# Seven products in place of eight for three of eight k-tile pairs in the first two column blocks of the last gate projection

## The reference, cut to what matters

```python
h = x
xn = rms_norm(h, attn_norm); proj = xn @ W_in
h = h + concat(gated_deltanet(...), moba_attention(...)) @ W_o
hn = rms_norm(h, ffn_norm)
h = h + (silu(hn @ w_gate) * (hn @ w_up)) @ w_down        # 2048 x 5632 and back
gate = sigmoid(rms_norm(h, ple_norm) @ w_ple_gate)         # 2048 x 2048
h = h + gate * (p @ w_ple_proj)                            # p 256 x 256, w 256 x 2048
```

## Time and profile before

| | us |
|---|---|
| median of 3 runs | 1311.76 (1311.75 to 1312.54) |
| the profiled execution | 1312.5 |
| its span, first to last instruction | 1310.8 |
| TensorE busy | 1302.5 (99%) |
| VectorE busy | 1025.2 (78%) |
| ScalarE busy | 704.7 (54%) |

### The profile page before, as it was taken

One profiled execution on the slowest core, in us unless ns is written; L12 is line 12 of the kernel. 1 busy time (PEld: TensorE's weight loads), 2 busy tenths in 40 slices (PEclk: granted clock), 3 DMA queues, 4 the chain that ended last, 5 costly groups with the idle time before them and its releaser, 6 DMA issues.

```text
span 1310.8 us, 18558 instructions
## 1 busy us (share of the span) xinstructions
PE 1302.5 (99%) x6595; PEld 1076.9 (82%) x6595; DVE 1025.2 (78%) x1381; ACT 704.7 (54%) x937; POOL 53.7 (4%) x71
## 2 busy tenths in 40 slices
PE   9999999999999999999999999999999999999998
PEld 8788888887888887888888888888888888888887
DVE  6578886788586668889888988679888997968554
ACT  6576444543455565555555654445555555555643
POOL 4003000221000000000000000000000000000000
PEclk9999999999999999999999999999999999999999
DMA  8555554455434555665666556566666656556563
GB/s 271 177 174 164 159 147 129 145 149 152 144 119 145 177 177 164 205 211 184 194 198 207 192 193 216 185 211 184 198 205 209 190 182 209 193 178 208 193 199 139
DMA packets 126204, 238.37 MB, mean 182 GB/s; under 512 B 9711, under 2 KB 10786, under 8 KB 126138
## 3 DMA queue, kind: packets, MB, share of 16 engines
q1 hardware_dynamic: 126106, 237.48, 56.8%
q10 hardware_dynamic: 32, 0.01, 0.0%
HBM read 235.36 MB, written 2.10 MB: 181 GB/s over the span
## 4 chain that ended last, share of the span: by engine, by line
PE 98%; DVE 1%; ACT 0%; issue 0%; DMA 0%; DVEq 0%; ACTq 0%
PE pair L627 16%; PE pair L629 16%; PE pair L628 16%; PE pair L908 11%; PE pair L909 11%; PE pair L910 11%; PE bg L908 2%; PE bg L909 2%; PE bg L910 2%; PE bg L748 2%; PE bg L818 2%; PE bg L685 1%; PE bg L903 1%; PE bg L799 0%; PE bg L660 0%; DVE w_lo L1493 0%
## 5 line engine op out<-in xcount | busy, mean ns | idle before, releaser
L1493 DVE TENSOR_TENSOR w_lo<-raw,w_hi 128x1024 fp32r<-128x1024 f32 x442 | 531.8, 1222 | 179.2 <-ACT w_hi L1099 177.4
L1099 ACT ACTIVATE w_hi<-raw 128x1024 fp32r<-128x1024 f32 x401 | 417.1, 1055 | 250.5 <-PE pair L629 139.9
L627 PE MATMUL pair<-w_hi,xT_hi 128*128 128x512 f32 x780 | 314.6, 403 | 0.0
L629 PE MATMUL pair<-w_hi,xT_lo 128*128 128x512 f32 x780 | 305.0, 391 | 0.0
L628 PE MATMUL pair<-w_lo,xT_hi 128*128 128x512 f32 x780 | 304.4, 390 | 0.0
L629 PEld LDWEIGHTS pair<-w_hi,xT_lo 128*128 128x128 f32 x780 | 146.5, 188 | 31.5
L627 PEld LDWEIGHTS pair<-w_hi,xT_hi 128*128 128x128 f32 x780 | 146.9, 188 | 28.9
L628 PEld LDWEIGHTS pair<-w_lo,xT_hi 128*128 128x128 f32 x780 | 147.0, 188 | 27.4
L1373 ACT ACTIVATE w_hi<-raw 128x1024 fp32r<-128x1024 f32 x41 | 43.6, 1062 | 134.7 <-DVE raw L1823 134.7
L908 PE MATMUL pair<-w_hi,actT_hi 128*128 128x512 f32 x296 | 115.9, 392 | 0.0
L910 PE MATMUL pair<-w_hi,actT_lo 128*128 128x512 f32 x296 | 115.3, 389 | 0.0
(11 more groups left out here) (351 smaller groups left out, 1886.0 us busy)
## 6 DMA issues: line engine op xcount, KB each, us to landing
raw<-in_w_in_dram SPq DMA_DIRECT2D x112, 512.0 KB, 3.7
raw<-in_w_gate_dram SPq DMA_DIRECT2D x88, 512.0 KB, 4.6
raw<-in_w_up_dram SPq DMA_DIRECT2D x88, 512.0 KB, 4.5
raw<-in_w_down_dram SPq DMA_DIRECT2D x88, 512.0 KB, 4.8
raw<-in_w_o_dram SPq DMA_DIRECT2D x32, 512.0 KB, 3.9
raw<-in_w_ple_gate_dram SPq DMA_DIRECT2D x32, 512.0 KB, 4.1
raw<-in_w_ple_proj_dram SPq DMA_DIRECT2D x4, 512.0 KB, 4.1
h<-in_x_dram SPq DMA_DIRECT2D x3, 512.0 KB, 8.0
```

The source lines that it names most:

```text
L627: mm(banks[t][:], hi[:, ts], wh, start=first, stop=False)
L629: m = mm(banks[t][:], lo[:, ts], wh, start=False, stop=last)
L1099: f(w_hi[j % RING][:], raw[j % RING][:], ACT.Copy).then_inc(hi_ready, 1)
L1493: v.tensor_tensor(w_lo[j % RING][:], raw[j % RING][:], w_hi[j % RING][:].bitcast(F32), ALU.subtract).then_inc(lo_ready, 1)
```

## The change

Groups 4, 5 and 6 of the gate projection's first two column blocks are computed with seven products for each pair of units. The units of these blocks come in the order `PG_SEQ`: block 0 groups 0, 1, 2, 3, 7 (G0 to G4), then the pair of group 4 for both blocks (G5, G6), block 1 group 0, the pair of group 5 (G8, G9), block 1 group 1, the pair of group 6 (G11, G12), block 1 groups 2, 3, 7 (G13 to G15). Blocks 2 and 3 stay plain. The steps hB of groups 4, 5 and 6 get the longer form with sums and differences. Those of groups 4 and 5 move from `U_PP - 2` to P1 (`U_PP + 1`). The sums of block 0 and of block 1 are finished at G12 and G15, and the multiply and add behind the sigmoid at G13 and G17.

```diff
-            at[(U_DB + FF_B * 8 // KU + 3, U_DB + FF_B * 8 // KU + 5, U_PP - 2, U_PP + 3)[n]][g].append(("hB", 2 * n + g))
+            at[(U_DB + FF_B * 8 // KU + 3, U_DB + FF_B * 8 // KU + 5, U_PP + 1, U_PP + 3)[n]][g].append(("hB", 2 * n + g))
...
+PG_MIXED = (4, 5, 6)
+PG_PLAIN = [g for g in range(UPB) if g not in PG_MIXED]
+PG_SEQ = ([(0, g) for g in PG_PLAIN] + [(0, PG_MIXED[0]), (1, PG_MIXED[0]), (1, PG_PLAIN[0])]
+          + [(0, PG_MIXED[1]), (1, PG_MIXED[1]), (1, PG_PLAIN[1])]
+          + [(0, PG_MIXED[2]), (1, PG_MIXED[2])] + [(1, g) for g in PG_PLAIN[2:]])
+PG_END = PG_SEQ.index((1, PG_MIXED[-1]))
...                                                     SyncE
+            for j, (side, g) in enumerate(PG_SEQ):
+                if j >= RING and PG_SEQ[j - RING] in [(0, m) for m in PG_MIXED]:
+                    sp.wait_ge(t4_ready, MIX_PG + PG_MIXED.index(PG_SEQ[j - RING][1]) + 1)
+                    fetch(j, w_pg, KU * g, side * CB)
+                else:
+                    load(U_PG + j, j, w_pg, KU * g, side * CB)
...                                                     TensorE, a mixed pair
+                    if first:
+                        pe.wait_ge(pair_free[1], 2 * ((B_PG + 1) // 2))
+                        for n in PG_MIXED:
+                            wait_read(pe, ("hB", n))
...
+                    use(u)
+                    product(bg[0][:], xT_hi[:, k0, a0], xT_lo[:, k0, a0], gh[:, 0, :], gl[:, 0, :], first, last)
+                    product(pair[0][0][:], xT_hi[:, k1, a0], xT_lo[:, k1, a0], gh[:, 1, :], gl[:, 1, :], False,
+                            last).then_inc(unit_used, 1)
+                    use(u + 1)
+                    product(bg[3][:], E_hi[:, q, 0, :], E_lo[:, q, 0, :], uh[:, 0, :], ul[:, 0, :], first, last)
+                    product(pair[1][0][:], E_hi[:, q, 2, :], E_lo[:, q, 2, :], uh[:, 1, :], ul[:, 1, :], first,
+                            False).then_inc(unit_used, 1)
+                    pe.wait_ge(t3_lo_ready, MIX_PG + q + 1)
+                    product(bg[2][:], E_hi[:, q, 3, :], E_lo[:, q, 3, :], t_hi[:, 2, :], t_lo[:, 2, :], first, last)
+                    pe.wait_ge(t24_lo_ready, MIX_PG + q + 1)
+                    product(bg[1][:], E_hi[:, q, 1, :], E_lo[:, q, 1, :], t_hi[:, 0, :], t_lo[:, 0, :], first, last)
+                    product(pair[0][1][:], xT_hi[:, k1, a1], xT_lo[:, k1, a1], t_hi[:, 1, :], t_lo[:, 1, :], False,
+                            last).then_inc(t_used, 1)
...                                                     ScalarE, step hB of groups 4, 5, 6
+                        if b - 1 in groups:
                             wait_read(act, (step, b - 1))
+                        elif step == "hB":
+                            act.wait_ge(down_sum, 4 * SUMS)
...                                                     (two scaled copies to xg as in hA)
+                        if step == "hB":
+                            f(xT_hi[:, 2 * b:2 * b + 2, :], xg[:], ACT.Copy).then_inc(x_hi, 2)
+                            act.wait_ge(form_ready, 4 * (c + 1))
+                            f(E_hi[:, q, :, :], F_raw[:], ACT.Copy).then_inc(form_rounded, 1)
+                            return
...                                                     ScalarE, the turns of P0 to G31
+                if side and g in PG_MIXED:
+                    split_mixed(u + LEAD, u + LEAD, MIX_PG + PG_MIXED.index(g) + 1, False)
+                elif u + LEAD < UNITS:
                     split(u + LEAD, u + LEAD)
                 for k in range(2):
                     for s in AT[u][k]:
...
                 if u < U_PG:
                     pp_end(u - U_PP)
                     continue
+                if u == U_PG + PG_END:
+                    act.wait_ge(t_used, MIX_PG + len(PG_MIXED))
+                    f(act_s[1][:], bg[0][:], ACT.Copy).then_inc(p1_copied, 1)
+                    for t in range(NT):
+                        act.wait_ge(gate_sum, 2 * (FF_A + FF_B) + t + 1)
+                        f(gate_s[t][:], gate_s[t][:], ACT.Sigmoid, scale=h_rs[1][:, t:t + 1]).then_inc(pair_free[0], 1)
...                                                     VectorE, step hB (behind F_raw as in hA)
+                        if step == "hB":
+                            v.tensor_tensor(xT_lo[:, 2 * b:2 * b + 2, :], xg[:], xT_hi[:, 2 * b:2 * b + 2, :].bitcast(F32), ALU.subtract)
+                            dve.wait_ge(form_rounded, c + 1)
+                            read_out(s, v.tensor_tensor(E_lo[:, q, :, :], F_raw[:], E_hi[:, q, :, :].bitcast(F32), ALU.subtract))
+                            return
...                                                     VectorE, the sums
+                if u == U_PG + PG_END:
+                    dve.wait_ge(p1_copied, done + 4 + 1)
...                                                     (six adds of 128 x 512: v_s, gate_s[0], u_s, gate_s[1], v_s, u_s)
+                if u == U_PG + PG_END + 1:
+                    finish(0, gate_s, pair_free[0], 2 * (B_PG // 2))
+                if u == U_PG + 2 * UPB - 1:
+                    wait_block(dve, u)
+                    dve.wait_ge(pg_parts, 2)
+                    for t, part in ((0, v_s), (1, u_s)):
+                        v.tensor_tensor(act_s[t][:], pair[1][t][:], part[:], ALU.add).then_inc(pair_free[1], 1)
+                if u == U_PG + 2 * UPB + 1:
+                    finish(1, act_s, pg_sig, 0)
```

More of the change, by code:

```diff
@@ L504, in _ @@
                 load(U_PP + b, b, w_pp, 0, b * CB)
-            with sp.Fori(0, 2) as i:
-                for j in range(2 * UPB):
-                    load(i * (2 * UPB) + (U_PG + j), j, w_pg, KU * (j % UPB), i * (2 * CB) + j // UPB * CB)
+            for j, (side, g) in enumerate(PG_SEQ):
[4 more added lines that the diff above has]
+                    load(U_PG + j, j, w_pg, KU * g, side * CB)
+            for j in range(2 * UPB, 4 * UPB):
+                load(U_PG + j, j, w_pg, KU * (j % UPB), j // UPB * CB)
             for b in range(3):
@@ L1053, in _ @@
                 down(ud, bd, n, n0, md, turn_last)
[L1055 to L1059, removed]
-            straight(U_PP, B_PP, 4, 1, lambda b, k: (pT_hi[:, k, :], pT_lo[:, k, :]))
-            straight(U_PG, B_PG, 3, UPB, normed)
+            straight(U_PP, B_PP, 4, 1, lambda b, k: (pT_hi[:, k, :], pT_lo[:, k, :]))
@@ new lines, in _ @@
+            a0, a1 = slice(0, P), slice(P, TOK)
+            pe.wait_ge(pair_free[0], 2 * (B_PG // 2))
+            for j, (side, g) in enumerate(PG_SEQ):
+                u = U_PG + j
+                k0, k1 = KU * g, KU * g + 1
+                if not side:
+                    wait_read(pe, ("hB", g))
+                if g in PG_MIXED:
+                    if side:
+                        continue
+                    q = PG_MIXED.index(g)
+                    first, last = q == 0, q == len(PG_MIXED) - 1
+                    if first:
+                        pe.wait_ge(pair_free[1], 2 * ((B_PG + 1) // 2))
+                        for n in PG_MIXED:
+                            wait_read(pe, ("hB", n))
+                    gh, gl = w_hi[j % RING], w_lo[j % RING]
+                    uh, ul = w_hi[(j + 1) % RING], w_lo[(j + 1) % RING]
+                    use(u)
[12 more added lines that the diff above has]
+                            last).then_inc(t_used, 1)
+                    continue
+                use(u)
+                for kk in range(KU):
+                    k = KU * g + kk
+                    wh, wl = w_hi[j % RING][:, kk, :], w_lo[j % RING][:, kk, :]
+                    end = side == 1 and j == len(PG_SEQ) - 1 and kk == KU - 1
+                    o = pair[side]
+                    product(o[0][:], xT_hi[:, k, a0], xT_lo[:, k, a0], wh, wl, not side and k == 0, end)
+                    last = product(o[1][:], xT_hi[:, k, a1], xT_lo[:, k, a1], wh, wl, k == 0, end)
+                    if kk == KU - 1:
+                        last.then_inc(unit_used, 1)
@@ L1064, in _ @@
+            straight(U_PG + 2 * UPB, B_PG + 2, 1, UPB, lambda b, k: (xT_hi[:, k, :], xT_lo[:, k, :]))
             last_pair = pair[(B_PG + 3) % 2]
@@ L1127, in post @@
                         act.wait_ge(x1_full, 1)
-                    if step == "hA" and b in MIXED:
-                        if b - 1 in MIXED:
+                    if b in {"hA": MIXED, "hB": PG_MIXED}.get(step, ()):
+                        groups = MIXED if step == "hA" else PG_MIXED
+                        if b - 1 in groups:
                             wait_read(act, (step, b - 1))
+                        elif step == "hB":
+                            act.wait_ge(down_sum, 4 * SUMS)
                         for kk in range(2):
@@ L1134, in post @@
                               scale=gains[:, col + k:col + k + 1]).then_inc(xg_ready, 1)
-                        q = MIXED.index(b)
-                        act.wait_ge(xg_ready, 2 * (q + 1))
+                        q = groups.index(b)
```

(55 more changed lines are left out.)

13 lines of the change are left out of this document (9 added, 4 removed).

## The result

| | us |
|---|---|
| median before | 1311.76 (6 runs, 1311.19 to 1312.54) |
| median after | 1317.17 (6 runs, 1316.0 to 1317.64) |
| ratio | 1.0042, 95% interval 1.0032 to 1.0051 |
| profiled execution after, its span | 1316.99, 1315.3 |

Slower, by 5.4 us; 4.06 were forecast. 1317.17 lies above the forecast's own range (1314.9 to 1316.7), inside the range for all (1313.2 to 1317.8), and nearest to rival C's 1317.5. The page of the kernel after, busy time and the last chain, against the earlier trace rows: nine matmuls fewer, and TensorE's share of the chain is 97% where it was 98%.

The account below looks back on a forecast made before the run. TensorE was taken to bound the kernel, its work and waits counting one for one. Terms -2.04 (matmuls) + 4.4 (wait) + 1.7 (clock) = +4.06 us gave 1315.8 us, own range 1314.9 to 1316.7, for all 1313.2 to 1317.8.

Parts of the forecast that it names:

- the forecast's own range: Whole kernel: 1314.9 to 1316.7 us around the forecast 1315.8, for start of the posts, handovers and clock; chance 0.65.
- the range for all: Whole kernel: 1313.2 to 1317.8 us over forecast and rivals, leaving out the no-wait rival and the slowest end.
- rival C: Behind P3's wait or at the sums: low clock twice as long, or waits at the sums; 1317.5 us, chance 0.15.
- What bounds the kernel: Whole kernel: TensorE, busy 1302.5 of 1310.8 us; work removed or waits added count one for one.
- Nine matmuls, 2.04 us: Gate phase's three mixed pairs: seven products instead of eight drop 9 matmuls of 0.2267 us, saving 2.04 us.
- The wait of 4.4 us: TensorE at P3's start: waits 4.4 us for ScalarE's copy of P1's banks behind two longer posts; bounds 2.2 and 6.7.
- The clock: Behind the wait at P3: TensorE's clock falls to half, losing 1.7 us more; bounds 0 and 3.4.
- my bound of 3.4 us: Behind the wait at P3: upper bound on the clock loss, low for twice the time.
- Splits and sums at nothing: Gate phase behind P3: VectorE's splits and sums keep ahead of TensorE; cost nothing, at most 0.5 us.
- The thinnest spot: Sums before G17: VectorE needs 10.2 us, TensorE wants G17 at 10.9; 0.7 us of cover.
- A (no wait): P3's start: ScalarE's copy comes in time, only the 9 matmuls count; 1309.7 us, chance 0.1.
- B (clock up): Behind P3's start: the wait comes but the clock stays at 2.4 GHz; 1314.1 us, chance 0.1.

Follow-up runs that it names:

- move only: Also called e3: kernel before the change, with hB steps of groups 4 and 5 moved to P1 in short form, eight products everywhere; 1311.77 us, ratio 0.9999.
- e4: Changed kernel with ScalarE's copies ahead of the posts, group 4's step three units before P0, group 5's behind P1's first k tile; 1310.29 us, ratio 0.9987.
- e10: The spread version of the changed kernel with only groups 4 and 5 through seven products, group 6 plain; 1310.89 us, ratio 0.9992.
- e9: Changed kernel with group 4's step three units before P0, ScalarE's copies still behind the posts; 98.58 us from P0 to the end.
- filler kernel with 18 matmuls: Changed kernel with 18 unused 512-column matmuls into a spare bank between P2 and P3; 1313.71 us, ratio 1.0014.
- 4 fillers: Changed kernel with 4 matmuls, results unused, in TensorE's gap ahead of P3; 1315.46 us, ratio 1.0027.
- e1: Changed kernel with ScalarE's copies of P units' banks put ahead of the hB posts of the same turn; 1313.66 us, ratio 1.0012.

## Why the prediction was right, and which term was too small

- **What bounds the kernel** held: TensorE's matmuls and its waits went into the time one for one. What came on top was the clock, and some tenths: 0.13 to 0.15 us for a restart behind a gap, 0.12 in "move only".
- **Nine matmuls, 2.04 us.** Shown by e4 (-1.98 us locally) and e10 (0.68 for each group).
- **The wait of 4.4 us.** 4.40 measured, twice. Step by step: the first post began 5.89 us after zero (5.9 to 6.1 forecast), the second 3.91 later (3.46 + 0.4), the copy 2.58 behind that (2.5), and ended 13.44 (13.45). VectorE's w_lo of G0 did hold up the first forms, to 7.18 us, 0.42 behind 5.89 + 0.87. e3 and e9 show that the length of the posts makes the wait, not the move.
- **The clock** fell, as forecast. Here a size was wrong: the term of 1.7 us. P3 took 2.90 us longer where I had 1.68, about 2.75 of it clock and 0.15 the restart. I had taken the loss from the one gap of half the length in the trace, where the clock was low for 3.4 us, all but a few hundredths of it behind the restart. Behind the new gap it was low for 6.8 us, in both profiles, of which 6.0 and 5.3 us lay behind the restart. That is the case of my bound of 3.4 us, "low for twice the time", and of the first half of rival C, which I had given 0.15. The sum with 2.90 in place of 1.7 is -2.04 + 4.40 + 2.90 = 5.26, and 5.40 were measured; 0.12 of the rest is in "move only" too.
- **Splits and sums at nothing.** No wait for a split behind P3. The thinnest spot came out at the forecast 0.7 us: VectorE ended w_lo of G17 at about 1269.07, TensorE began G17 at 1269.75. In e4, with no standstill ahead to let VectorE catch up, 0.46 us were left (1261.72 and 1262.18): enough, but near its end.

VectorE in order of time, the turns of G16 and G17 in the kernel after (the last row is w_lo of G17 and of G18), where the earlier trace rows had the same four instructions:

```profile
1264.05 1.22 DVE L1569 TENSOR_TENSOR w_lo<-raw,w_hi 128x1024 fp32r<-128x1024 f32 x1 [0.55 <-ACT w_hi L1154]
1265.19 0.68 DVE L2037 TENSOR_TENSOR gate_s<-gate_s,pp 128x512 f32<-128x512 f32 x1
...
1267.24 0.69 DVE L2039 TENSOR_TENSOR h<-h,gate_s 128x512 f32<-128x512 f32 x1
1267.85 2.35 DVE L1569 TENSOR_TENSOR w_lo<-raw,w_hi 128x1024 fp32r<-128x1024 f32 x2
```

- **The rivals.** A (no wait) fell: the copy came 4.4 us late. B (clock up) is what the filler kernel with 18 matmuls gives, +2.62 us, and what the changed kernel did not do in either profile. C was right in its first half: the low clock lasted for twice as long (6.8 against 3.4 us), and its 1317.5 is 0.3 us from the median of 1317.17, the forecast's 1315.8 is 1.4 away. Its second half, waits at the sums, did not come. So the direction and the wait were right for the reason given, and the time came out inside the range for all because the bound for the clock was wide enough, not because 1.7 us was the right size.

What stays open: why the clock was low for 6.8 us behind some gaps and for 3.4 behind others, when it falls, before or behind the restart, and how often it does so behind a gap of a given length.

## What to carry to other kernels

When a step moves in an engine's queue, look at what stands behind it in the same turn and who waits for that: here a 1.1 us copy, with 0.97 us of cover, was pushed back by two posts of 6.49 us together, in which ScalarE stands idle for a third of the time, waiting for VectorE. Measure such a post from its start to the next work behind it, not by the sum of its instructions. Price a gap in TensorE's stream twice, once for the wait and once for the clock, and the second as a range: here gaps of 2.2 to 4.25 us cost nothing to 2.8 us of clock, and those of 1.1 to 2.0 us none, in one profile each.

## What the runs showed of the hardware that was not expected

The same gap of 2.2 us lets the granted clock fall to 0.50 in some executions of the same code and not in others, which is worth 1.7 us and a good part of the spread of the kernel before (33 runs from 1310.65 to 1313.15 us; the 12 below 1311.9 have a mean clock of 1.000 but for two, the 21 above 0.998 to 0.999). The fall can come after TensorE has resumed: 1.4 us behind the start of P3 with 4 fillers, 1.0 us behind that of G0 in e1; in the two profiles of the changed kernel it came 0.8 and 1.5 us ahead of the restart. The Trainium skill ("TensorE: Matmul & The Clock Gate", Part 1: The HAM clock gate) says that activity is what releases the throttle and that the point at which the clock rises at the start of sustained work varies between runs. The rows agree with the first (it rose again with TensorE at work, 6.0 and 5.3 us behind the restart), and show such a variation for the fall.
